# Three attentions on one core: which engine scales which row of the exponentials

## What is computed

```python
def one_block(q_blk):
    s = jnp.einsum('bqkgd,bskd->bkgqs', q_blk, k).astype(jnp.float32) * scale
    p = jax.nn.softmax(s, axis=-1).astype(v.dtype)
    return jnp.einsum('bkgqs,bskd->bqkgd', p, v)
```

## Time and profile before

| | us |
|---|---|
| median of 3 runs | 2651.66 |
| lowest and highest of them | 2650.67, 2652.53 |
| the profiled execution | 2654.48 |
| its span in the trace | 2653.2 |
| layer a's steps, from the first score to the last turn | 147.0 to 220.8 |
| layer b's | 783.3 to 857.8 |
| layer c's | 1365.8 to 1457.8 |

### The profile page before, as it was taken

The page is one execution under the profiler, slowest core; times in us unless marked ns, Lnnn a source line. Parts: engine busy times, 40 slices in busy tenths (PEclk is TensorE's granted clock), DMA queues, the critical chain, the costliest instruction groups (busy, mean ns, idle before and its releaser), DMA issues.

```text
span 2653.2 us, 33052 instructions
## 1 busy us (share of the span) xinstructions
PE 2579.4 (97%) x13418; PEld 2084.4 (79%) x13418; DVE 1288.4 (49%) x2151; ACT 979.5 (37%) x1620; POOL 1255.2 (47%) x618
## 2 busy tenths in 40 slices
PE   8989999999998999999999999999999999999999
PEld 5667888888776888888766888888788888888887
DVE  4863799842035399992557341222345233431221
ACT  4464423223347332232458342232324222432231
POOL 4865444444447444444468344444343444344442
PEclk9999999999999999999999999999999999999999
DMA  4201555532220366552210233322432222333322
GB/s 145 64 17 49 181 188 182 188 117 75 95 80 2 95 196 198 186 165 96 72 49 2 64 111 96 95 95 80 163 96 83 81 94 80 95 96 95 96 96 79
DMA packets 259436, 274.48 MB, mean 103 GB/s; under 512 B 6869, under 2 KB 249301, under 8 KB 259029
## 3 DMA queue, kind: packets, MB, share of 16 engines
q1 hardware_dynamic: 259284, 272.37, 31.9%
HBM read 270.26 MB, written 2.10 MB: 103 GB/s over the span
## 4 chain that ended last, share of the span: by engine, by line
PE 84%; DVE 8%; POOL 4%; issue 2%; ACT 1%; DMA 0%; SPq 0%; DVEq 0%
PE bank L452 22%; PE bank L453 22%; PE bank L454 22%; DVE acc L1362 2%; PE bank L520 2%; PE bank L522 2%; PE bank L521 2%; PE bank L428 2%; PE bank L429 2%; DVE tmp L1397 2%; PE bank L432 2%; POOL PA L1740 1%; POOL PBB L1740 1%; PE bank L584 1%; PE bank L624 1%
## 5 line engine op out<-in xcount | busy, mean ns | idle before, releaser
L1706 POOL TENSOR_TENSOR wlo<-raw,whi 128x1024 fp32r<-128x1024 f32 (+1 forms) x408 | 988.8, 2445 | 1193.9 <-ACT whi L900 1193.8
L452 PE MATMUL bank<-Xhi,whi 128*128 128x512 f32 (+1 forms) x1616 | 640.4, 396 | 1.4 <-POOL wlo L1706 1.4
L453 PE MATMUL bank<-Xlo,whi 128*128 128x512 f32 (+1 forms) x1616 | 629.9, 390 | 0.0
L454 PE MATMUL bank<-Xhi,wlo 128*128 128x512 f32 (+1 forms) x1616 | 629.1, 389 | 0.0
L900 ACT ACTIVATE whi<-raw 128x1024 fp32r<-128x1024 f32 (+1 forms) x408 | 404.9, 1041 | 570.0 <-PE bank L454 495.6
L452 PE MATMUL bank<-Hhi,whi 128*128 128x512 f32 x1024 | 400.6, 391 | 0.0
L453 PE MATMUL bank<-Hlo,whi 128*128 128x512 f32 x1024 | 398.9, 390 | 0.0
L454 PE MATMUL bank<-Hhi,wlo 128*128 128x512 f32 x1024 | 398.4, 389 | 0.0
L452 PEld LDWEIGHTS bank<-Xhi,whi 128*128 128x128 f32 (+1 forms) x1616 | 302.3, 187 | 73.0 <-issue 8.1
L453 PEld LDWEIGHTS bank<-Xlo,whi 128*128 128x128 f32 (+1 forms) x1616 | 302.4, 187 | 65.0 <-issue 3.2
L454 PEld LDWEIGHTS bank<-Xhi,wlo 128*128 128x128 f32 (+1 forms) x1616 | 302.4, 187 | 65.0
(11 more groups left out here) (269 smaller groups left out, 3146.6 us busy)
## 6 DMA issues: line engine op xcount, KB each, us to landing
ada<-in_ada_w SPq DMA_DIRECT2D x48, 1024.0 KB, 5.3
raw<-in_w_up SPq DMA_DIRECT2D x32, 1024.0 KB, 5.7
raw<-in_w_down SPq DMA_DIRECT2D x32, 1024.0 KB, 5.0
raw<-in_mlp_w_in SPq DMA_DIRECT2D x32, 1024.0 KB, 5.6
raw<-in_mlp_w_out SPq DMA_DIRECT2D x32, 1024.0 KB, 5.2
raw<-in_gmlp_w_in SPq DMA_DIRECT2D x24, 1024.0 KB, 5.0
raw<-in_gmlp_w_out SPq DMA_DIRECT2D x12, 1024.0 KB, 5.0
raw<-in_w_in_a SPq DMA_DIRECT2D x8, 1024.0 KB, 5.2
```

The costliest lines, as they stand in the source:

```text
L452: pe.matmul(b[0:rows, :], whi[s][:, c, j:j + rows], hi[:, c, :], start=(c == 0), stop=False)
L453: pe.matmul(b[0:rows, :], whi[s][:, c, j:j + rows], lo[:, c, :], start=False, stop=False)
L454: m = pe.matmul(b[0:rows, :], wlo[s][:, c, j:j + rows], hi[:, c, :], start=False, stop=(c == KC - 1))
L1706: pool.tensor_tensor(wlo[u % 2][:, c0:c1, 0:k], src[:, c0:c1, 0:k], whi[u % 2][:, c0:c1, 0:k].bitcast(F32), ALU.subtract).then_inc(lo_done, 1)
```

## The change

Before, the even steps have one row scaled by VectorE and one by GpSimd, and the odd steps both by GpSimd. After it, the even steps have both rows scaled by GpSimd, and the odd ones the first by VectorE and the second by GpSimd. The number of scales of each engine stays, 16 and 48 in each attention. The counts in `scaled_by` follow, and the very first `turn` no longer waits for VectorE.

```diff
     def scaled_by(a, n):
 
-        return 16 * ATT[a] + n // 2 + 1, 48 * ATT[a] + n + 1 + (n + 1) // 2
+        return 16 * ATT[a] + (n + 1) // 2, 48 * ATT[a] + n + 2 + n // 2
...
                 by_dve, by_pool = scaled_by(a, n)
-                pe_until.wait_ge(pn_dve, by_dve)
+                if n:
+                    pe_until.wait_ge(pn_dve, by_dve)
                 pe_until.wait_ge(pn_pool, by_pool)
...
-                    if n % 2:
+                    if n % 2 == 0:
                         dve_until.wait_ge(rc_done, base // 2 + n)
                         dve.tensor_scalar(p[:, 0:w], p[:, 0:w], both[:, 0, 2:3], None, ALU.mult).then_inc(pn_dve, 1)
...
-                for r in (2 * n, 2 * n + 1)[1 - n % 2:]:
+                for r in (2 * n, 2 * n + 1)[n % 2:]:
```

## The result

| | us |
|---|---|
| before, median of 8 runs beside the changed kernel | 2650.56 (2647.58 to 2655.3) |
| changed, median of 8 | 2657.27 (2654.57 to 2659.95) |
| ratio, 95% interval | 1.0025 (1.0014 to 1.0036) |
| profiled execution before and after, spans | 2653.2 and 2657.7 |

The changed kernel is slower by some 6.7 us, 0.25%. The range of 2649.0 to 2659.0 held the time. The likeliest case, "within 0.2%" at 2653.5, did not: the difference is a little over the bound, in the case that had 0.18, though the interval reaches from 0.14% to 0.36% and so lies on both sides of it. The prediction took 0.2% for about what can't be told from none; the interval is half as wide to each side.

What follows compares the result with a forecast made beforehand. The prediction took waits through GpSimd's scales as the bound, with the change shifting it to the ring through i2. Ring turns, heads and tails summed to +1.8 us on the 2651.66 median, about 2653.5 us, range 2649.0 to 2659.0.

Steps and rivals of the forecast that it cites:

- within 0.2%: Whole kernel: forecast 2653.5 us, a difference under 0.2% (5.3 us), about indistinguishable from none; chance 0.77.
- the case that had 0.18: Whole kernel slower than 2657.0 us, by rival 1 or a slower thing not seen; chance 0.18.
- The ring through both rows of i2: Third of a group's four steps i0 to i3: GpSimd's pair, ScalarE, VectorE and back, 8.90 us in a and b, 11.44 in c.
- the sum: All three layers, ring turns plus head and tail: a +0.4, b -0.8, c +2.2, together +1.8 us.
- the base: Ring through i2 in a group before contention between scales: 8.80 us in a and b, 11.18 in c.
- collision: VectorE's scale of i3 falls into GpSimd's pair of i2: +0.10 us a group in a and b, +0.26 in c.
- the row at 1378.90: Profile before: VectorE's scale began 0.80 us into a GpSimd scale, three scales took 4.83 instead of 4.64 us, +0.19.
- Rival 1: VectorE's scale of i3 and GpSimd's pair of i2 lock each other out, mostly in a and b: 2657.7 us; chance 0.14.
- The prediction's own sign of being wrong: A chain still with i3 in a, groups under 8.6 or over 9.1 us, or VectorE scales over 0.7 us.
- the row at 1406.41: Profile before: VectorE's scale began half a us into a GpSimd scale and took 0.49 us, no contention.
- Head and tail: Each layer's first steps and end: heads -0.4 in a, -0.15 in b, +1.9 in c; tails -0.55, -0.55, -0.8 us.
- Rival 2: Relief of odd steps is real and the i2 ring has unseen slack: -21 us, 2630; chance 0.05.

Runs made afterwards that it cites:

- thin_i2: Changed kernel with GpSimd's second scale of step i2 cut to one column: 2637.04 us in one run, groups of 8.21, 8.34 and 10.77 us.
- no_i3: Changed kernel with VectorE's scale of step i3 cut to one column: 2650.75 us in one run, groups 8.85 us in a and b, 11.19 in c.
- oneport: Changed kernel with VectorE's scale of step i3 in the form that also writes an accumulator: 2652.05 us in one run, groups 8.86, 8.86 and 11.20.
- only_c: New order in layer c alone, a and b as before the change: 2654.45 us, ratio 1.0012 (1.0003 to 1.0021).
- only_ab: New order in layers a and b alone, c as before the change: 2653.05 against 2650.68 us, ratio 1.0008 (1.0000 to 1.0017).
- changed again: The changed kernel unaltered, measured and traced a second time: 2657.28 against 2650.15 us before, ratio 1.0027 (1.0017 to 1.0036).
- c_head: New order in layer c alone, but VectorE scales the first row of c's very first step: 2652.64 against 2650.15 us, ratio 1.0011.
- no_i1: Changed kernel with VectorE's scale of step i1 cut to one column: 2653.74 us in one run, groups 8.88 in a, 10.92 in c.
- each: VectorE scales the first row of every step and GpSimd the second, in all layers: 2635.05 against 2650.53 us before, ratio 0.9944.

## Why the prediction was right, and where it was not

**The mechanism was right.** The ring through both rows of i2, ScalarE's copy, the high part, VectorE and back is the chain of all three layers after the change, and `thin_i2` shows that it is the cause. The range held in part by its width: the sum came to +1.8 us, and the medians are 6.7 apart.

**The terms of the ring.** Forecast 8.90, 8.90 and 11.44 us; measured 9.01, 9.01 and 11.43. In a and b the base was 8.80 and is 8.85 (`no_i3`; a turn that waits for GpSimd releases ScalarE 0.66 us later, not 0.60). In c base and collision were right, 11.18 and 0.26 against 11.19 and 0.24. The mis-sized term is the collision: half of the row at 1378.90 was taken, 0.10, and it is 0.16, nearly the whole of that row's 0.19. But it isn't that row's case: there VectorE's scale kept its 0.48 us and GpSimd's running scale was longer, here VectorE's is held and GpSimd's next one is longer. Over six turns the two terms make 0.7 us in a and as much in b. The effect in a settled group of b had its sign wrong (+0.10, not -0.01).

**Rival 1.** It came out at 2657.7 and the kernel at 2657.3, which is luck. GpSimd's pair of i2, in a and in c:

```profile
191.77 1.24 POOL L1741 TENSOR_SCALAR PA<-PA,stats 128x384 f32<-128x384 f32 x1 [0.80 <-DVE stats L1343]
...
192.99 1.40 POOL L1741 TENSOR_SCALAR PA<-PA,stats 128x384 f32<-128x384 f32 x1
...
1422.46 1.80 POOL L1741 TENSOR_SCALAR PC<-PC,stats 128x512 f32<-128x512 f32 x1
```

VectorE's scale of i3 begins 0.81 us into GpSimd's first scale of i2 (191.77, 192.58) and takes 0.71 us instead of 0.49. So it does wait, as the rival said, but only 0.22 us, not to the end of that scale, 0.43. GpSimd's second scale takes 0.16 longer, not 0.30 to 0.36. The prediction's own sign of being wrong, a VectorE scale of over 0.7 us, did show, if barely: the lock is there in part. It does not last for the whole of a GpSimd scale. In the kept traces a 512-wide scale of VectorE that begins 0.70 to 0.96 us into a 384-wide one of a GpSimd pair ends 1.52 to 1.53 us behind the start of that one, whenever it began, so by its free 0.49 us it was let in at some 1.04, an estimate, 0.2 before the end.

"Fully blocks" is the rule of the Trainium skill's "SBUF — State Buffer", section "SBUF: two separate sides". Under "Who interferes with whom" in that section the Trainium skill leaves out the form that also writes its accumulator, and there `oneport` agrees: that form collides with nothing. On the whole instruction the traces don't agree: 0.22 us were waited and not 0.43, and the row at 1406.41 shows a plain scale that begins in the middle of GpSimd's and isn't held at all.

**Head and tail.** For c the head was forecast at +1.9 and is +2.2, the tail at -0.8 and is -0.8 (from the reciprocal of step 30 to the last transposes 6.40 us before, 5.56 after). For a and b the head was forecast at -0.4 and -0.15. This step failed in a, and in both it lacked a term, TensorE's clock. The reciprocals counted from the first score of the layer, in us:

| | a, step 6 | a, step 30 | b, step 6 | b, step 30 | c, step 10 | c, step 30 |
|---|---|---|---|---|---|---|
| before | 16.2 | 68.2 | 15.5 | 69.0 | 29.2 | 85.3 |
| `only_c` | 15.9 | 67.9 | 14.0 | 67.5 | 31.3 | 88.2 |
| `only_ab` | 14.9 | 69.0 | 15.3 | 69.4 | 29.1 | 85.3 |
| changed | 16.6 | 70.7 | 15.3 | 69.4 | 31.3 | 88.2 |
| changed again | 16.6 | 70.7 | 15.3 | 69.4 | 31.3 | 88.3 |

`only_c` and the kernel before run the same order in b, and b's head is 1.5 us apart. The granted clock tells them apart: in the head of b before, and in `only_c` (columns as above):

```profile
788.00:794.00 6.00, 4.95 (x48) 3.35 (x49) 3.81 (x18) 4.14 (x15) 5.79 (x5) 0.64 0.00 0
794.00:800.00 6.00, 5.72 (x64) 4.02 (x64) 3.33 (x17) 4.44 (x13) 2.77 (x3) 0.79 0.01 4
```

```profile
786.40:792.40 6.00, 3.78 (x54) 2.58 (x56) 4.30 (x22) 4.14 (x16) 6.00 (x6) 1.00 0.00 0
792.40:798.40 6.00, 5.71 (x78) 4.34 (x78) 2.70 (x13) 5.27 (x17) 4.02 (x4) 1.00 0.02 4
```

The trace that the prediction rested on had a slow head of b, 0.64 and 0.79 of the clock, where the old order in `only_c` and `c_head` kept 1.00; with the new order the clock fell at that place in both traces of the changed kernel and in `only_ab`. I had left the clock out of the sum altogether. At like clocks the forecast for b was fair: step 6 of b comes at 15.5 in the old order and 15.3 in the new with the clock fallen, and at 14.0 in the old and 13.6 in `no_i3` (which has one scale less) with the clock at 1.00. But against a b that keeps its clock the change costs 1.3 us, where the table's first line shows a gain of 0.2. Of the traces with the old order in b one of three has the fall, of those with the new one (the changed kernel twice, `only_ab`, `oneport`, `no_i1`, `no_i3`) five of six; what decides it was not tried.

In a the clock falls in every trace, but from 12 to 15 us behind the first score it is back at 1.00 in four of them (`only_ab`, `oneport`, `thin_i2`, `each`) and at 0.53 to 0.65 in the other eight, of either order. `only_ab` has step 6 at 14.9, the changed kernel twice at 16.6: identical instructions in a, and 1.7 us apart. With the long fall the new order is 0.4 to 0.7 us later than the old, not 0.4 sooner.

**The sum.** The forecast was worked out on the profiled execution, 2654.5 to 2656.3, and that of the changed kernel took 2659.0: +4.5, not +1.8. From its first score to its last transpose the three layers add up to 239.9 us before and 244.3 after, and all the rest takes 2413.3 and 2413.4. By layer:

| | forecast | measured | turns of the ring | head | tail |
|---|---|---|---|---|---|
| a | +0.4 | +2.3 | 2.0 | 0.4 | -0.2 |
| b | -0.8 | +0.1 | 0.6 | -0.2 | -0.3 |
| c | +2.2 | +2.1 | 0.8 | 2.2 | -0.8 |

That is 2.7 us too little: 1.1 in the ring (2.4 against 3.5), 0.8 in the heads of a and b, 0.3 in c's, 0.5 in the tails. (In the second trace of the changed kernel the tail of a is -0.7.)

The medians are 6.7 and 7.1 apart, 2.2 and 2.6 more. The profiled execution before was a slow one of its kind, 3.9 us over its median, the changed one 1.8 over. 1.5 us of this is the head of b with its clock fallen (15.5 against 14.0), which makes 5.9. The last us is inside the intervals. The rest of the program, which the change doesn't touch, takes 2410.4 to 2413.4 us in the kept traces, so it can hide there; whether it comes from the clock was not tried and stays open. The median that I started from, 2651.66 of three runs, was itself a us above the 2650.2 to 2650.7 of the larger groups.

**Rival 2** named the right prize for the wrong kernel. A group can get shorter by much more than any ring that this change touched, once no step has two GpSimd rows: 15.5 us in `each`.

## What to carry to other kernels

In a loop in which engines hand work round, look for each ring and not for the engine with the most work: a load moved off the ring that binds lands on another, and the longer of the two sets the new time. Two slow operations in a row that feed one waiting instruction cost twice; split every such pair over two engines, as `each` does, rather than choose which pair to keep. And before a gain or loss of a few us is read from one trace, compare the granted clock of the same stretch in a second one.

## What the runs showed of the hardware

- A VectorE scale that starts 0.81 us into a 1.24 us GpSimd scale takes 0.71 us instead of 0.49, and the GpSimd scale behind it 1.40 instead of 1.24; one that starts half a us into a 1.56 us scale takes 0.49 and delays nothing. What the two do to each other hangs on where in GpSimd's scale VectorE's begins. In the kept traces, with 512 columns on both: begun 0.18 to 0.46 us in, VectorE's ends at 0.96 to 0.97; begun 0.50 to 0.63 in, it takes its free 0.49; begun 0.96 to 1.35 in, it ends at 1.84 to 1.85 and GpSimd's next scale takes 1.73 instead of 1.56. Between these, at 0.71 and 0.80, VectorE's keeps 0.48 to 0.49 and GpSimd's running one takes 1.66 and 1.75. (Left out is `each`, where VectorE has already held up the GpSimd scale from its start.)
- The accumulating form of VectorE's scale takes 0.75 us at 512 columns, longer than the plain one alone (0.49) and beside GpSimd (0.71), and yet the group is shorter with it (8.86 against 9.01), since GpSimd's pair isn't held up.
- A short wait of TensorE at the start of a stage can be followed by a clock of 1.2 GHz for the microseconds behind it, as at c's head (0.68 us of work in 3, then a granted clock of 0.54). In a and b the same instructions came to the reciprocal of step 6 up to 1.7 and 1.5 us later where the clock was longer at its lower level.
